# RWKV scan: the transposed operands and the place of a chunk's decay

## The chip, the cores and the metric

The kernel runs on one core of one Trainium2 chip. The metric is the device time of one execution in microseconds; before the change it is 4066.91 us, the median of three runs (4065.96 to 4070.18).

## The reference, cut to what matters

The program is three model blocks one after the other. The change touches one part of the second block, a recurrence of the RWKV-7 kind over 512 tokens, run forward and backward over 16 heads of width 64. With a state S per head, a decay w, a key k, a "removal" key kk and gains b, what is computed per token is

```
S_t = diag(w_t) S_{t-1} - (S-side term built from kk_t and b_t) + k_t v_t^T
y_t = S_t^T r_t          (forward and backward results are added)
```

The kernel does this by chunks of 64 tokens. Inside a chunk everything becomes products of matrices. From chunk to chunk the state moves by one affine step, S' = phi S + psi. With D the product of the decays of a whole chunk, one value per row of the state, both forms below give the same step:

```
before:  phi = diag(D) + (tail operands)^T (...)      psi = (tail operands)^T (...)
after:   S' = D * ( (eye + (side operands)^T (...)) S )  +  D * ( (side operands)^T (...) )
```

A tail operand is k or b times the decay from its token to the end of the chunk; a side operand is k or b divided by the decay up to its token. The first is D times the second.

## The kernel before

`rwkv_projection` makes the operands; at its end it also prepares the first half of the scan (`first_half`), beside its matmuls. `rwkv_scan` then runs 16 halves: u = 0 to 15, tile u // 2 of 128 channels (two heads), forward where u is even and backward where it is odd. Each engine (PE, DVE, ACT) has its program as a loop over u, with the order of the steps written out by hand: the early work of half u is woven between the late work of half u - 1 (its state steps and outputs). I call one pass of that loop a turn and number it by u, so a forward turn has u even. An engine never goes past an instruction that waits, so the written order is also the order of time. `need(u, name, n)` waits for the n-th event of that name of half u.

What the change and the prediction touch, by lines:

- DVE `summed` L3264 (running sum of log decays), `exponents` L3273 (total minus running sum), `keys` L3282, `sides` L3288 and L3289 (`scan_KB`, the side operands), `rows_read` L3297, `past` L3432, `tails` L3304 and L3305 (`scan_hat`, the tail operands).
- DVE `masked` L3313: copies the Gram matrices out of PSUM, `scan_MH` for the first set (w = 0) and `scan_NG` for the second (w = 1). PE `grams` L2933 makes them.
- DVE `crossed` L3369 (`scan_Z`) and `carried` L3380 (`scan_X`), PE `crossed` L2972, `carried` L2984 and `turned` L2947: the doubling levels 3, 4 and 5 of the block inverse; ACT `turned` L3189 (`scan_Y`).
- DVE `substituted` L3350 and L3353, and `blocks_placed` L3362, which starts the doubling of half u.
- PE `tail_rows` L2915: transposes of `scan_hat`, which ACT copies to `scan_tok`; PE `values` L3086.
- PE `transitions` L3021 to L3027, DVE `transitions` L3389 (phi), ACT `decay_diagonals` L3172 (`scan_diag`), ACT `offsets` L3181 (psi).
- PE `state_step` L3062 and DVE `state_step` L3421, six times per half; PE `within` L3040 to L3046 lies between the first and the second of them, and PE `turned(u, 2)` L2947 behind the second.

The order on PE from the Gram matrices to the start of the doubling is: `grams(u, 0)`, `carried(u-1, 5)`, `tail_rows(u)`, `values(u)` (forward only), `turned(u-1, 5)`, `solved(u-1)`, `grams(u, 1)`, `spread_blocks(u)`, `transitions(u-1)`, `values_carried(u)`, `bonus_sums(u)` (forward only), `state_step(u-1, 1)`, `within(u-1)`, `state_step(u-1, 2)`, `turned(u, 2)`. The end of a turn on DVE is `keys`, `crossed(u, 4)`, `sides`, `carried(u, 4)`, `rows_read`, `past`, `tails`, `crossed(u, 5)`, and the next turn opens with `masked(u+1, 0)`, then `carried(u, 5)`.

Of the kernel before, what the change touches and what calls it, by code (L numbers as in the profile page):

```python
# [14 lines left out]
P = 128  # L15
SEQ = 512
# [2370 lines left out]
def rwkv_projection(G, T):  # L2387
# [17 lines left out]
    with ExitStack() as ctx:  # L2405
# [4 lines left out]
                  "scanned", "opened", "exponents", "inverse_exp", "exps", "prepared", *(f"staged_out_{m}" for m in range(KT)))  # L2410
# [153 lines left out]
        def _(act):  # L2564
# [62 lines left out]
            for s in range(KT + 1, STEPS):  # L2627
# [14 lines left out]
                if s == 2 * KT + 3:  # L2642
                    act.wait_ge(S["exponents"], 1)
                    act.activation(T.pe_end[:, FWD, :], F[:, RW_CHUNK - 1::RW_CHUNK], ACT.Exp, scale=DECAY_SCALE)
                    act.activation(inv, F, ACT.Exp, scale=-DECAY_SCALE).then_inc(S["inverse_exp"], 1)
                if s == 2 * KT + 4:
                    act.activation(upto(grown), by_chunk(F), ACT.Exp, scale=DECAY_SCALE)
                    act.activation(upto(left), upto(left), ACT.Exp, scale=DECAY_SCALE).then_inc(S["exps"], 1)
# [5 lines left out]
        def _(dve):  # L2654
# [36 lines left out]
            def first_half(m):  # L2691
# [5 lines left out]
                if m == 2:  # L2697
                    total = F[:, RW_CHUNK - 1::RW_CHUNK]
                    total = bass.AP(tensor=total.tensor, offset=total.offset, ap=[total.ap[0], total.ap[1], [0, RW_CHUNK]])
                    dve.wait_ge(S["scanned"], 1)  # L2700
                    dve.tensor_tensor(upto(left), total, by_chunk(F), ALU.subtract).then_inc(S["exponents"], 1)
# [6 lines left out]
                if m == 6:  # L2708
# [4 lines left out]
                    dve.tensor_tensor(by_chunk(T.hat[:, 0, :]), by_chunk(ld[:, 1, :]), upto(left), ALU.mult)  # L2713
                if m == 7:
                    dve.tensor_tensor(by_chunk(T.hat[:, 1, :]), by_chunk(ld[:, 3, :]), upto(left), ALU.mult)
# [75 lines left out]
def rwkv_scan(G, T):  # L2791
# [11 lines left out]
    PER = dict(scanned=1, exponents=1, edge=1, sums_read=2, exps=1, keys_ready=1, rows_ready=1, sides_ready=1, tails_ready=1, token_sum=3, token_done=3, gram_sum=4, gram_done=4,  # L2803
               z_sum=3, z_done=3, x_sum=3, x_done=4, y_sum=4, y_done=4,
               block_masked=3, compacted=1, unit=1, spread_sum=1, spread_done=1, product=SUB - 1, small=SUB - 1, nv_sum=1, nv_done=1,
               ua_sum=2, ua_done=2, diag_done=1, phi_sum=2, phi_done=2, psi_done=2, own_sum=1, own_done=1, read_done=1,
               state_sum=6, state_done=6, past_sum=1, past_done=1)
    PER_TURN = dict(decays_loaded=16, loaded=16, bonus_in=1, bonus_sum=1, bonus_done=1, bonus_stored=16, v_sum=1, v_done=1)
    with ExitStack() as ctx:
# [4 lines left out]
        AR, KB, hat, masks, bonus, pe_end = T.AR, T.KB, T.hat, T.masks, T.bonus, T.pe_end  # L2814
        diag = G.sb("scan_diag", [P, 2, N_CHUNKS, RW_N], ctx=ctx)
# [46 lines left out]
        def _(sp):  # L2862
# [5 lines left out]
            for i in range(KT):  # L2868
                if i == 1:
                    sp.wait_ge(S["v_spilled"], 16 * 2)  # L2870
                if i:
# [6 lines left out]
                    need(2 * i - 1, "tails_ready", 1)  # L2878
# [8 lines left out]
        def _(pe):  # L2887
# [17 lines left out]
            def tail_rows(u):  # L2905
# [144 lines left out]
            def state_step(u, n):  # L3050
# [76 lines left out]
        def _(act):  # L3127
            need = needer(act)

            def decays(u):  # L3130
# [3 lines left out]
                need(u, "exponents", 1)  # L3134
                ends = F[:, RW_CHUNK - 1::RW_CHUNK]
                if d == FWD:
                    act.sem_inc(S["edge"], 1)
                else:
                    act.activation(left[:, :, 0:1], ends.rearrange("p (c t) -> p c t", t=1), ACT.Copy).then_inc(S["edge"], 1)
                act.activation(pe_end[:, d, :], ends, ACT.Exp, scale=DECAY_SCALE).then_inc(S["sums_read"], 1)  # L3140
                act.activation(upto(grown), by_chunk(F), ACT.Exp, scale=DECAY_SCALE)
                need(u, "edge", 1)
                act.activation(by_chunk(inv), by_chunk(F) if d == FWD else ahead(left), ACT.Exp, scale=-DECAY_SCALE).then_inc(S["sums_read"], 1)
                need(u, "sums_read", 2)
                of = upto(left) if d == FWD else left
                act.activation(of, of, ACT.Exp, scale=DECAY_SCALE).then_inc(S["exps"], 1)
# [18 lines left out]
            def decay_diagonals(u):  # L3165

# [8 lines left out]
            def offsets(u):  # L3175
                if not 0 <= u < HALVES:
                    return
                d = u % 2
# [44 lines left out]
            act.sem_inc(S["edge"], 1)  # L3223
            act.sem_inc(S["sums_read"], 2)
            act.sem_inc(S["exps"], 1)
            for u in range(-1, HALVES + 1):
# [11 lines left out]
                decay_diagonals(u)  # L3238
# [4 lines left out]
        def _(dve):  # L3243
# [22 lines left out]
            def exponents(u):  # L3266
                if not 0 <= u < HALVES:
                    return
# [30 lines left out]

            def tails(u):  # L3300
                if not 0 <= u < HALVES:
                    return
# [1360 lines left out]
```

## Time and profile before

| | us |
|---|---|
| median of three runs | 4066.91 |
| the profiled execution | 4058.67 |
| its span | 4057.3 |
| PE busy | 3854.9 (95%) |
| DVE busy | 2282.2 (56%) |
| ACT busy | 1318.3 (32%) |
| the scan, from the first masked Gram matrix to its last output | 1777 to 2170 |

The scan is 393 us of the span, about a tenth. A share of busy time is a mean over stages that are limited by different engines, so what the change is worth can be read only inside these 393 us, and there from what each engine waits for. Of the views used below, the one by stretch gives busy time and granted clock, the one of waits gives who waited for whom, the one of groups gives the mean duration of a kind of instruction, and the instructions in order of time show which wait ends last. An idle time in brackets stands behind the instruction that ended it, with what released it.

### The profile page before, as it was taken

Reading aid. Unit: us, or ns where it says so; the run is one execution under the profiler, and the core shown is the slowest. Engines: PE = TensorE matmul, PEld = TensorE weight load, DVE = VectorE, ACT = ScalarE, POOL = GpSimd, SP = SyncE. Lnnn points to the kernel's source line nnn. Section 1 sums busy time; section 2 is a strip of 40 time slices with the busy share of each in tenths; the row PEclk is TensorE's granted clock in tenths of the full one; section 3 lists DMA queues with packets and bytes.
Section 4 is the critical chain, followed back from the end, with each engine's and each line's share of the span. In section 5 each row is a group of like instructions: output and inputs, shape, how many; then the busy total and the mean of one; then the engine's idle time right before and its main releaser. Section 6 shows DMA issues by size and latency. Waiting matters only on the chain. (4 is left out here: it accounts for less than half of the span.)

```text
span 4057.3 us, 63395 instructions
## 1 busy us (share of the span) xinstructions
PE 3854.9 (95%) x26412; PEld 3044.2 (75%) x26412; DVE 2282.2 (56%) x3290; ACT 1318.3 (32%) x2121; POOL 1348.0 (33%) x550
## 2 busy tenths in 40 slices
PE   8999999999999999988888999999999999999998
PEld 6856788876778887577775788777777787877886
DVE  5746477567677665568884776465550626251033
ACT  3246233343223332444443433322222112103222
POOL 1001444443234441000001444355554343654442
PEclk9999999999999999999998999999999999999998
DMA  5310222232112223441112222222122112222221
GB/s 176 125 50 35 93 94 99 88 132 104 62 63 104 103 83 111 160 151 45 49 45 87 83 89 98 90 83 83 67 79 75 66 63 90 88 104 83 101 86 62
DMA packets 43375, 359.85 MB, mean 89 GB/s; under 512 B 4307, under 2 KB 4691, under 8 KB 23804
## 3 DMA queue, kind: packets, MB, share of 16 engines
q1 hardware_dynamic: 43132, 356.35, 24.3%
q8 instruction: 184, 3.01, 0.3%
q14 instruction: 59, 0.48, 0.0%
HBM read 333.79 MB, written 22.28 MB: 88 GB/s over the span
## 5 line engine op out<-in xcount | busy, mean ns | idle before, releaser
L352 POOL TENSOR_TENSOR ffn_weights_low<-weight_ring,ffn_weights_high 128x2048 fp32r<-128x2048 f32 x128 | 591.8, 4624 | 787.3 <-ACT ffn_weights_high L451 786.6
L202 PE MATMUL banks<-ffn_in_high,ffn_weights_low 128*128 128x512 f32 x2048 | 800.8, 391 | 12.8 <-POOL ffn_weights_low L352 8.8
L203 PE MATMUL banks<-ffn_in_low,ffn_weights_high 128*128 128x512 f32 x2048 | 798.2, 390 | 0.0
L204 PE MATMUL banks<-ffn_in_high,ffn_weights_high 128*128 128x512 f32 x2048 | 798.2, 390 | 0.0
L202 PEld LDWEIGHTS banks<-ffn_in_high,ffn_weights_low 128*128 128x128 f32 x2048 | 385.4, 188 | 98.9 <-POOL ffn_weights_low L352 11.3
L204 PEld LDWEIGHTS banks<-ffn_in_high,ffn_weights_high 128*128 128x128 f32 x2048 | 385.3, 188 | 80.6
L203 PEld LDWEIGHTS banks<-ffn_in_low,ffn_weights_high 128*128 128x128 f32 x2048 | 385.3, 188 | 80.0 <-issue 0.7
L451 ACT ACTIVATE ffn_weights_high<-weight_ring 128x2048 fp32r<-128x2048 f32 x128 | 245.2, 1915 | 560.0 <-PE banks L204 560.0
L605 DVE SCALAR_TENSOR_TENSOR ffn_gate<-ffn_up,columns_sb,ffn_gate 128x511 f32<-128x511 f32 (+1 forms) x132 | 273.6, 2072 | 160.8 <-ACT ffn_value L495 160.8
L3764 POOL TENSOR_TENSOR third_weights_low<-weight_ring,third_weights_high 128x1024 fp32r<-128x1024 f32 x144 | 359.8, 2498 | 11.5
L3762 POOL CAST third_weights_high<-weight_ring 128x1024 fp32r<-128x1024 f32 x144 | 159.4, 1107 | 512.4 <-PE banks L204 483.4
L202 PE MATMUL banks<-third_x_high,third_weights_low 128*128 128x512 f32 x768 | 311.5, 406 | 2.0 <-DVE merge_gate L4582 0.9
L204 PE MATMUL banks<-third_x_high,third_weights_high 128*128 128x512 f32 x768 | 300.6, 391 | 0.0
L203 PE MATMUL banks<-third_x_low,third_weights_high 128*128 128x512 f32 x768 | 300.1, 391 | 0.0
L626 DVE TENSOR_TENSOR ffn_in_low<-ffn_hidden,ffn_in_high 128x512 fp32r<-128x512 f32 x80 | 165.9, 2121 | 138.4 <-ACT ffn_in_high L509 138.4
L3528 POOL TENSOR_TENSOR rwout_weights_low<-weight_ring,rwout_weights_high 128x1024 fp32r<-128x1024 f32 x8 | 18.6, 2361 | 615.6 <-ACT rwout_weights_high L3579 615.6
L202 PEld LDWEIGHTS banks<-third_x_high,third_weights_low 128*128 128x128 f32 x768 | 145.1, 189 | 32.5 <-issue 3.1
L204 PEld LDWEIGHTS banks<-third_x_high,third_weights_high 128*128 128x128 f32 x768 | 144.7, 188 | 31.1
L203 PEld LDWEIGHTS banks<-third_x_low,third_weights_high 128*128 128x128 f32 x768 | 145.2, 189 | 27.8 <-issue 1.0
L202 PE MATMUL banks<-first_in_high,first_weights_low 128*128 128x512 f32 x336 | 139.5, 415 | 15.7 <-DVE first_in_low L1105 12.5
L498 ACT ACTIVATE ffn_gate<-ffn_gate 128x512 f32<-128x512 f32 x66 | 41.8, 634 | 320.3 <-DVE ffn_gate L605 320.3
L618 DVE TENSOR_TENSOR ffn_hidden<-ffn_gate,banks 128x512 f32 (+1 forms) x22 | 15.2, 689 | 215.7 <-ACT ffn_gate L500 215.7
(646 smaller groups left out, 7474.4 us busy)
## 6 DMA issues: line engine op xcount, KB each, us to landing
weight_ring<-weights SPq DMA_DIRECT2D x144, 2048.0 KB, 7.7
scan_in<-rwkv_operands SPq DMA_DIRECT2D x7, 1280.0 KB, 5.8
rwkv_operands<-rwin_staged SPq DMA_DIRECT2D x23, 256.0 KB, 3.3
scan_in<-rwkv_operands SPq DMA_DIRECT2D x8, 512.0 KB, 3.9
bias_tiles<-bias_rows SPq DMA_DIRECT2D x8, 448.0 KB, 8.9
residual<-x SPq DMA_DIRECT2D x4, 512.0 KB, 7.1
hyena_u_x_T<-decay SPq DMA_DIRECT2D x2, 1024.0 KB, 8.0
rwkv_residual<-residual SPq DMA_DIRECT2D x1, 2048.0 KB, 7.2
```

The costliest lines, as they stand in the source:

```text
L202: pe.matmul(out, w[1], x[0], start=start, stop=False, skip_group_check=True)
L203: pe.matmul(out, w[0], x[1], start=False, stop=False, skip_group_check=True)
L204: return pe.matmul(out, w[0], x[0], start=False, stop=stop, skip_group_check=True)
L352: pool.tensor_tensor(parts[1], landed, parts[0].bitcast(F32), ALU.subtract).then_inc(S["split"], 1)
L451: act.activation(parts[0], landed, ACT.Copy).then_inc(S["rounded"], 1)
L498: act.activation(gc[:, h, :], gc[:, h, :], act_func).then_inc(S["activated"], 1)
L605: ins = dve.scalar_tensor_tensor(out=buf[:, h, to], in0=up_scaled[:, h, q, of], scalar=G.col(taps, 8 * t + 4 * q + tap), in1=buf[:, h, to] ...
L618: dve.tensor_tensor(gT[:, t, :], gc[:, h, :], G.banks[:, b + 1, :], ALU.mult).then_inc(S["hidden"], 1)
L626: dve.tensor_tensor(parts[1], gT[:, t, :], parts[0].bitcast(F32), ALU.subtract).then_inc(S["tile_split"], 1)
L3528: pool.tensor_tensor(w_parts[1][:, k, :], landed(k), w_parts[0][:, k, :].bitcast(F32), ALU.subtract).then_inc(S["split"], 1)
L3762: pool.tensor_copy(parts[0], landed).then_inc(S["rounded"], 1)
L3764: pool.tensor_tensor(parts[1], landed, parts[0].bitcast(F32), ALU.subtract).then_inc(S["split"], 1)
```

## The change

The side operands are transposed in place of the tail operands, so `tails` and the tile `scan_hat` go, as do the forward half's `exponents` and the exponential that fed it. `scan_diag` and the eight ACT instructions that fill it go; phi is now formed by adding the plain identity. The chunk's decay D (`pe_end`) enters at two places: ACT copies psi in eight pieces of 64 columns, each scaled by its chunk's D, where it copied two pieces of 256; and each DVE state step becomes (product times D) plus psi, a three-operand instruction. PE's first state step now waits for five pieces of psi. In `rwkv_projection` the same tail work of the first half goes.

```diff
-                need(u, "tails_ready", 1)
+                need(u, "sides_ready", 1)
                 if u > 1:
-                    need(u - 2, "psi_done", 2)
+                    need(u - 2, "psi_done", N_CHUNKS)
...
-                        mm = pe.transpose(B(d, 2 + n)[:, j * P:(j + 1) * P], hat[:, n, j * P:(j + 1) * P], G.con("ident"))
+                        mm = pe.transpose(B(d, 2 + n)[:, j * P:(j + 1) * P], KB[:, n, j * P:(j + 1) * P], G.con("ident"))
...
                 if n == 1:
                     need(u, "phi_done", 2)
-                    need(u, "psi_done", 2)
+                    need(u, "psi_done", N_CHUNKS // 2 + 1)
...
-                for c in range(N_CHUNKS):
-                    ins = act.activation(diag[:, d, c, :], eye, ACT.Copy, scale=pe_end[:, d, c:c + 1])
-                ins.then_inc(S["diag_done"], 1)
...
-                for p in range(2):
-                    need(u, "phi_done", p + 1)
-                    act.activation(psi[:, p::2, :], B(d, 2 + p)[:, 256:512].rearrange("p (j k) -> p j k", j=JT), ACT.Copy)\
+                for c in (*order[d][1 - d::2], *order[d][d::2]):
+                    need(u, "phi_done", 2 - c % 2)
+                    at = 256 + c // 2 * RW_N
+                    act.activation(psi[:, c, :], B(d, 2 + c % 2)[:, at:at + RW_N], ACT.Copy, scale=pe_end[:, u % 4, c:c + 1])\
                        .then_inc(S["psi_done"], 1)
...
             def exponents(u):
-                if not 0 <= u < HALVES:
+                if not 0 <= u < HALVES or u % 2 == FWD:
...
-            def tails(u):
-                if not 0 <= u < HALVES:
-                    return
-                behind = upto(left) if u % 2 == FWD else ahead(grown)
-                dve.tensor_tensor(by_chunk(hat[:, 0, :]), by_chunk(k), behind, ALU.mult)
-                dve.tensor_tensor(by_chunk(hat[:, 1, :]), by_chunk(b), behind, ALU.mult).then_inc(S["tails_ready"], 1)
...
-                need(u, "diag_done", 1)
-                for p in range(2):
+                for p in (1, 0):
                     need(u, "phi_sum", p + 1)
-                    dve.tensor_tensor(phi[:, p::2, :], B(d, 2 + p)[:, 0:256].rearrange("p (j k) -> p j k", j=JT), diag[:, d, p::2, :], ALU.add)\
+                    dve.tensor_tensor(phi[:, p::2, :], B(d, 2 + p)[:, 0:256].rearrange("p (j k) -> p j k", j=JT), spread(eye, JT), ALU.add)\
...
-                if n == 1:
-                    need(u, "psi_done", 2)
-                dve.tensor_tensor(state[:, d, n + 1, :], B(d, 3)[:, n * RW_N:(n + 1) * RW_N], psi[:, order[d][n], :], ALU.add)\
-                   .then_inc(S["state_done"], 1)
+                need(u, "psi_done", N_CHUNKS // 2 + 1 + n // 2)
+                c = order[d][n]
+                dve.scalar_tensor_tensor(out=state[:, d, n + 1, :], in0=B(d, 3)[:, n * RW_N:(n + 1) * RW_N], scalar=pe_end[:, u % 4, c:c + 1],
+                                         in1=psi[:, c, :], op0=ALU.mult, op1=ALU.add).then_inc(S["state_done"], 1)
```

ACT's `decays` for a forward half loses the last of its exponentials; `pe_end` gets four slots in place of two; an unused tile of the size of `scan_hat` keeps the addresses of what follows. The loads of the next tile's operands (SP) no longer wait for the tail operands.

## Rows read from the trace of the kernel before

**Rows 1.** Busy time by stretch, whole scan: PE, PEld, DVE, ACT, POOL, clock, DMA share, GB/s.

```profile
1777.00:2170.00 393.00, 322.75 (x10427) 277.69 (x10420) 304.40 (x792) 173.44 (x430) 1.36 (x1) 0.93 0.15 52
```

**Rows 2.** Waits, 1800 to 2150: us in total, times, longest us.

```profile
DVE scan_state L3421 <- PE banks L3062: 26.6, 34, 2.0
...
PE banks L3062 <- ACT scan_psi L3181: 8.5, 7, 1.4
...
PE banks L3062 <- issue: 4.5, 8, 1.3
```

**Rows 3.** In order of time, into backward turn 7: start us, us, engine, line.

```profile
1941.87 1.08 PE L2933 MATMUL banks<-scan_AR,scan_KB 64*64 64x128 f32 x32
...
1942.06 0.68 DVE L3305 TENSOR_TENSOR scan_hat<-scan_in,residual 128x512 f32<-128x512 f32 x1
1942.67 0.42 DVE L3369 TENSOR_TENSOR scan_Z<-banks,scan_masks_sb 128x256 f32<-128x256 f32 x1
...
1943.01 1.29 DVE L3313 TENSOR_TENSOR scan_MH<-banks,scan_masks_sb 128x512 f32<-128x512 f32 x2
...
1944.21 0.41 DVE L3380 TENSOR_TENSOR scan_X<-scan_X,banks 128x256 f32<-128x256 f32 x1
```

**Rows 4.** In order of time, the same place in forward turn 8.

```profile
1963.04 1.10 PE L2933 MATMUL banks<-scan_AR,scan_KB 64*64 64x128 f32 x32
...
1964.49 0.67 PE L2984 MATMUL banks<-scan_Z,scan_Y 64*64 64x32 f32 x32 [0.34 <-DVE scan_Z L3369]
...
1965.54 0.41 DVE L3380 TENSOR_TENSOR scan_X<-scan_X,banks 128x256 f32<-128x256 f32 x1
...
1966.45 0.60 PE L2947 MATMUL banks<-constants_sb,scan_X 128*128 128x128 f32 x4
```

**Rows 5.** In order of time, turn 7, the second set of Gram matrices.

```profile
1947.01 1.09 PE L2933 MATMUL banks<-scan_AR,scan_KB 64*64 64x128 f32 x32
...
1947.54 0.69 DVE L3273 TENSOR_TENSOR residual<-residual 128x512 f32<-128x512 f32 x1
...
1948.15 1.29 DVE L3313 TENSOR_TENSOR scan_NG<-banks,scan_masks_sb 128x512 f32<-128x512 f32 x2
```

**Rows 6.** In order of time, DVE: the first masked Gram matrix of the scan.

```profile
1777.39 1.29 DVE L3313 TENSOR_TENSOR scan_MH<-banks,scan_masks_sb 128x512 f32<-128x512 f32 x2 [9.89 <-PE banks L2933]
```

**Rows 7.** Groups on ACT by shape, the scan: count, busy us, mean ns.

```profile
L3189 ACT ACTIVATE scan_Y<-banks 128x512 f32<-128x512 f32 x64 | 38.2, 597 | 106.8 <-PE banks L2947 106.8
L3172 ACT ACTIVATE scan_diag<-scan_masks_sb,scan_decay 128x64 f32<-128x64 f32 x128 | 32.1, 336 | 0.0
...
L3181 ACT ACTIVATE scan_psi<-banks 128x256 f32<-128x256 f32 x32 | 10.7, 396 | 3.4 <-DVE scan_phi L3389 3.4
```

**Rows 8.** In order of time, ACT: psi of one half, the diagonals of another.

```profile
1951.61 0.67 ACT L3181 ACTIVATE scan_psi<-banks 128x256 f32<-128x256 f32 x2
...
1959.29 2.00 ACT L3172 ACTIVATE scan_diag<-scan_masks_sb,scan_decay 128x64 f32<-128x64 f32 x8
```

**Rows 9.** In order of time, turn 7: first state step to the start of the doubling.

```profile
1952.38 0.33 PE L3062 MATMUL banks<-scan_psi,scan_phi 64*64 64x64 f32 x4 [1.36 <-ACT scan_psi L3181]
...
1953.69 0.68 DVE L3362 TENSOR_TENSOR scan_X<-scan_small,scan_masks_sb 128x512 f32<-128x512 f32 x1
...
1954.43 0.66 PE L2947 MATMUL banks<-constants_sb,scan_X 128*128 128x128 f32 x4 [0.15 <-DVE scan_X L3362]
```

**Rows 10.** In order of time, PE: the same place in turns 1 and 15.

```profile
1812.08 0.22 PE L3062 MATMUL banks<-scan_state,scan_phi 64*64 64x64 f32 x1
...
1812.39 0.66 PE L2947 MATMUL banks<-constants_sb,scan_X 128*128 128x128 f32 x4
...
2140.27 0.33 PE L3062 MATMUL banks<-scan_state,scan_phi 64*64 64x64 f32 x4
2140.53 0.66 PE L2947 MATMUL banks<-constants_sb,scan_X 128*128 128x128 f32 x4
```

**Rows 11.** In order of time, DVE: a three-operand instruction with a scalar per partition.

```profile
1954.45 0.74 DVE L3254 SCALAR_TENSOR_TENSOR scan_bonus<-scan_in,columns_sb 128x512 f32<-128x512 f32 x1
```

More of the change, by code:

```diff
@@ L2409, in rwkv_projection @@
                   "mixed_out", "gained_out", "key_in", "decays_in", "reset_in", "masks_in", "first_share", "first_key", "first_gain", "first_read",
-                  "scanned", "opened", "exponents", "inverse_exp", "exps", "prepared", *(f"staged_out_{m}" for m in range(KT)))
+                  "scanned", "opened", "inverse_exp", "exps", "prepared", *(f"staged_out_{m}" for m in range(KT)))
         sb = lambda name, shape, dt=F32: G.sb("rwin_" + name, shape, dt, ctx=ctx)
@@ L2642, in _ @@
                 if s == 2 * KT + 3:
-                    act.wait_ge(S["exponents"], 1)
-                    act.activation(T.pe_end[:, FWD, :], F[:, RW_CHUNK - 1::RW_CHUNK], ACT.Exp, scale=DECAY_SCALE)
+                    act.wait_ge(S["scanned"], 1)
+                    act.activation(T.pe_end[:, 0, :], F[:, RW_CHUNK - 1::RW_CHUNK], ACT.Exp, scale=DECAY_SCALE)
                     act.activation(inv, F, ACT.Exp, scale=-DECAY_SCALE).then_inc(S["inverse_exp"], 1)
                 if s == 2 * KT + 4:
-                    act.activation(upto(grown), by_chunk(F), ACT.Exp, scale=DECAY_SCALE)
-                    act.activation(upto(left), upto(left), ACT.Exp, scale=DECAY_SCALE).then_inc(S["exps"], 1)
+                    act.activation(upto(grown), by_chunk(F), ACT.Exp, scale=DECAY_SCALE).then_inc(S["exps"], 1)
             for m in range(KT):
@@ L2696, in first_half @@
                     dve.tensor_tensor_scan(F, G.x[:, RESET_TILE, :], ld[:, 5, :], 0.0, ALU.mult, ALU.add).then_inc(S["scanned"], 1)
[L2697 to L2701, printed above, removed]
                 if m == 5:
@@ L2813, in rwkv_scan @@
         NG = G.sb("scan_NG", [P, 2, 2, JT, 2, RW_CHUNK], ctx=ctx)
-        AR, KB, hat, masks, bonus, pe_end = T.AR, T.KB, T.hat, T.masks, T.bonus, T.pe_end
-        diag = G.sb("scan_diag", [P, 2, N_CHUNKS, RW_N], ctx=ctx)
+        AR, KB, masks, bonus, pe_end = T.AR, T.KB, T.masks, T.bonus, T.pe_end
         phi = G.sb("scan_phi", [P, N_CHUNKS, RW_N], ctx=ctx)
@@ L3133, in decays @@
                 d = u % 2
-                need(u, "exponents", 1)
                 ends = F[:, RW_CHUNK - 1::RW_CHUNK]
                 if d == FWD:
-                    act.sem_inc(S["edge"], 1)
+                    need(u, "scanned", 1)
+                    act.activation(pe_end[:, u % 4, :], ends, ACT.Exp, scale=DECAY_SCALE).then_inc(S["sums_read"], 1)
+                    act.activation(inv, F, ACT.Exp, scale=-DECAY_SCALE).then_inc(S["sums_read"], 1)
+                    act.activation(upto(grown), by_chunk(F), ACT.Exp, scale=DECAY_SCALE).then_inc(S["exps"], 1)
                 else:
+                    act.wait_ge(S["exponents"], u // 2 + 1)
                     act.activation(left[:, :, 0:1], ends.rearrange("p (c t) -> p c t", t=1), ACT.Copy).then_inc(S["edge"], 1)
[L3140 to L3146, printed above, removed]
+                    act.activation(pe_end[:, u % 4, :], ends, ACT.Exp, scale=DECAY_SCALE).then_inc(S["sums_read"], 1)
+                    act.wait_ge(S["edge"], u // 2 + 1)
+                    act.activation(by_chunk(inv), ahead(left), ACT.Exp, scale=-DECAY_SCALE).then_inc(S["sums_read"], 1)
+                    need(u, "sums_read", 2)
+                    act.activation(left, left, ACT.Exp, scale=DECAY_SCALE).then_inc(S["exps"], 1)
             def key_rows(u):
@@ L3237, in _ @@
                 turned(u, 3)
-                decay_diagonals(u)
                 key_rows(u + 1)
@@ L3440, in bonus_times_value @@
                    .then_inc(S["bonus_done"], 1)
-            for sem in ("keys_ready", "rows_ready", "sides_ready", "tails_ready", "bonus_in", "scanned", "exponents"):
+            for sem in ("keys_ready", "rows_ready", "sides_ready", "bonus_in", "scanned"):
                 dve.sem_inc(S[sem], 1)
@@ L3472, in _ @@
                 past(u - 1)
-                tails(u + 1)
                 crossed(u, 5)
```

21 lines of the change are left out of this document (6 added, 15 removed).

## The prediction

> **What bounds the kernel now.** I read the stretches first, to find the scan and its clock: in 393 us PE is busy for 323 and DVE for 304 [rows 1], so both are near full and neither share says which one a turn waits for. The reader is to see that "DVE at 77%" does not yet make DVE work worth removing. Then the waits: inside the scan DVE stands 26.6 us in 34 waits for the product of a state step, and PE waits for psi before its first state step in 7 turns, with 8 more where the profile names no releaser [rows 2]; in those 8 too PE's step starts 0.1 us after ACT's second psi copy ends, so all 15 full turns wait for psi there. Last, the instructions in order of time, at the three places that the change touches.
>
> The first place is the end of a turn. DVE finishes the tail operands, masks scan_Z and starts scan_MH at 1943.01, and PE's Gram matrices end at 1941.87 + 1.08 = 1942.95 [rows 3]. scan_MH starts 0.06 us behind the Gram matrices, which is what a release takes. So although DVE works without a gap, it is PE that lets it go on. I read the same pair at all turns: the distance is 0.01 to 0.11 in thirteen of the fifteen turns from 1 on, and 0.21 in turns 8 and 10. The second place is the second set of Gram matrices: PE ends them at 1948.10, scan_NG starts at 1948.15 [rows 5], and this distance is 0.02 to 0.08 in all sixteen. The third is the way from psi to the doubling: PE's step at 1952.38, then `within`, the second step, and the transposes that start the doubling [rows 9]. The loop that sets the time thus runs through PE and ACT, and through DVE in the substitution, the state steps and from the sixth step to the fourth-level scan_X.
>
> **The tail operands (L3304, L3305) go.** Two instructions of 0.68 that follow one another at 0.60 [rows 3]: 1.2 us of DVE in each turn. What they hold back is scan_Z of level 5 and what follows it. In a backward turn scan_MH can't start sooner than the Gram matrices end, and scan_X stands behind it on DVE (1944.21), so PE's transposes of scan_X, and all behind them, come no sooner: worth 0. In a forward turn PE has work of its own between (`tail_rows`, `values`): scan_X ends at 1965.95, but the transposes start at 1966.45 [rows 4], so here PE's queue counts, and it starts with `carried` at 1964.49, 0.34 us idle behind scan_Z. With scan_Z early it starts at about 1964.05, where the Gram matrices let it go: 0.45 gained. That is the most of the seven forward turns; in the least it is 0, since `carried` already follows the Gram matrices. I take half: 7 x 0.23 = 1.6 us gained; the bounds are 0 and 3.2.
>
> **The forward exponents (L3273) go**, 0.69 on DVE once in two turns, and stand ahead of scan_NG. scan_NG is released by PE [rows 5]: worth 0. The exponential that ACT loses there only makes ACT idle sooner. The transposes wait for the side operands in place of the tail operands; both are ready before PE gets there, and SP's load of the next tile is issued sooner, with nobody waiting for it.
>
> **In the projection** the same work goes. DVE then stands idle for 9.89 us until the first Gram matrices are there [rows 6]: worth 0.
>
> **The diagonals (L3172) go**, eight of 0.336 us, 2.0 together [rows 8], between two ACT copies with idle time before the next: worth 0. The identity in their place has the same shape on DVE: 0, and I see no reason for either sign.
>
> **Psi in eight pieces.** This is the part that lies on the path. Two copies take 0.67 from the start of the first to the end of the second [rows 8]. Now PE waits for five pieces. A piece has the shape and the scalar operand of a diagonal, 0.336 each, eight in 2.00, so one follows the other at (2.00 - 0.336) / 7 = 0.238, and the fifth ends after 4 x 0.238 + 0.336 = 1.29: 0.62 later than now. The other bound leaves the scalar operand out: from 597 at 512 elements and 396 at 256 [rows 7] a copy costs 0.785 ns per element, 0.245 at 64, following one another at about 0.13, so 0.77 in all: 0.10 later. I take 0.62, since the diagonal is the nearer row: same size, same scale operand, same engine, only its input is in SBUF.
>
> The Trainium skill (VectorE: DVE Perf Modes, the section on the TRN2 errata) speaks against this part: it says that the fixed cost is paid by every instruction, and that many small tiles pay it each time. The rows agree, since a quarter of the elements takes 336 against 396. The same section puts the fixed part lower when the input is in PSUM, and with its figures, plus what ScalarE: Activation LUTs (the section on what ACT_TABLE_LOAD costs) gives for a scalar operand per partition, I would estimate the fifth piece 0.4 later in place of 0.62, and the sum below 3 us lower.
>
> How much of it reaches the doubling? In turn 7 scan_X is placed at 1953.69 + 0.68 = 1954.37 and the transposes wait for it [rows 9]; PE had been ready 0.27 earlier, so 0.62 - 0.27 = 0.35 is left. Turns 2 and 11 look alike. In the other twelve PE is the late one: its transposes follow the second state step by 0.31 in turn 1 and 0.26 in turn 15, the first and the last of them [rows 10], and the whole 0.62 passes. Sum: 12 x 0.62 + 3 x 0.35 = 8.5; with the lower bound 12 x 0.10 = 1.2. What is late next is DVE's second step, its bonus and own output behind it, and then scan_Z of level 3: the same delay by another way, so none of it is given back. ACT itself is held 1.3 us longer by eight pieces; its next copy, scan_Y, stands idle for 106.8 us in 64 copies [rows 7], 1.7 each, and moves by 0.6 itself: I hold it covered, closely in the forward turns.
>
> **State steps with three operands.** Of this kind a 512-element instruction takes 0.74 [rows 11] against 0.68 without the scalar [rows 3]: 0.06 more each. A third of the steps make DVE wait for PE [rows 2] and others lie in DVE's full stretches; I take three of six on the path: 15 x 3 x 0.06 = 2.7; the bounds are 0 and 5.4. Nothing here excludes that the small size hides it.
>
> **The last pass**, half 15 alone, has nothing beside it: 0.62 + 6 x 0.06 = 1.0.
>
> **The sum**: - 1.6 + 8.5 + 2.7 + 1.0 = +10.6 us. The profiled execution took 4058.67 and would take 4069.3. It is 8.2 below the median of the runs, so I add the sum to the median: 4077.5. Some of PE's stalls without a releaser come from the supply of its instructions, I believe, and a longer wait just ahead of one may swallow part of it; I round down to 4077. The low bounds of the terms give -3.2 + 1.2 + 0.1 = -2, the high ones 8.5 + 5.4 + 1.0 = +15, that is 4065 to 4082.
>
> **The rivals.**
>
> A. DVE's relief counts after all (faster). If DVE and not PE were last at the end of a turn, each turn would win the 1.2 us of the tails and each second one 0.6 of the exponents: 15 x 1.2 + 7 x 0.6 = 22, less the 12 that the rest costs: -10, 4057. For it speaks that DVE shows no idle time through most turn ends; against it the distances of 0.06 and 0.05 [rows 3, 5]. It decides from the point where DVE ends its work there after PE in most turns, which it now does clearly in two.
>
> B. The psi pieces are cheap (same). If a piece costs what the lower bound says, and the state steps nothing more: 1.2 + 0.1 - 1.6 = -0.3, or +3 if the state steps do cost their 2.7 and 0.4: 4067 to 4070. For it: input in PSUM. Against it: the diagonals.
>
> C. PE's clock (slower by more). The granted clock is 0.93 in the scan [rows 1], which is 0.07 x 2 x 393 = 55 us at 1.2 GHz in place of 2.4. PE's wait before the first step, 1.36 in turn 7 [rows 9], grows by 0.6. If the time at 1.2 GHz grows by a quarter with it, 14 us at half the rate cost at most 7 more: 4084. It can also fall the other way.
>
> **How the numbers follow.** The forecast has 0.50, A 0.10, B 0.25, C 0.15. Range: the forecast's own 4065 to 4081, opened towards C above and halfway to A below: 4062 to 4087. A measurement can tell about 0.2%, 8.1 us, from no change, so "same" is 4058.8 to 4075.0. B lies in it whole, and of the forecast a quarter: 0.25 + 0.12 = 0.37; faster is A, 0.10; slower is the rest, 0.53.
>
> **What would show each step.** In the changed trace: scan_MH and scan_NG still start 0.05 behind the Gram matrices while DVE shows about 1 us of new idle time before them (if they start earlier than PE's end allows now, A). ACT's L3181 line has 128 instructions of 64 columns; their mean and the time from the first to the end of the fifth settle 0.10 against 0.62. PE's L3062 starts 0.1 behind the fifth piece, and its wait is some 0.6 longer. The state step's mean on DVE goes from 0.222 to about 0.28. The clock of 1777 to 2170 tells of C. I am wrong if the scan's 393 us [rows 1] fall, or if the time that moves lies outside them.

## The result, and the profile after

| | before | after |
|---|---|---|
| median of 17 runs each, us | 4066.84 | 4074.53 |
| the profiled execution's span | 4057.3 | 4066.4 |
| the scan, first scan_MH to the end of its last output | 389.8 | 397.4 |

The ratio is 1.0020, with a 95% interval of 1.0013 to 1.0027: 5 to 11 us slower, 7.7 between the medians. On another chip the same pair gave 1.0008 (0.9999 to 1.0018), 3.3 us between the medians. Within the profiled executions the scan takes 7.5 us longer. So DVE's and ACT's work went down and the time went up, by 0.1 to 0.3%. The forecast was +10.6, 4077.

The page of the changed kernel, busy time by engine:

```profile
PE 3857.2 (95%) x26412; PEld 3043.6 (75%) x26412; DVE 2265.5 (56%) x3250; ACT 1295.6 (32%) x2073; POOL 1347.2 (33%) x550
```

DVE works 16.7 us less, ACT 22.7 us less, PE 2.3 us more. The scan alone, by stretch, with the same columns as [rows 1]:

```profile
1775.52:2172.88 397.36, 320.68 (x10416) 279.70 (x10416) 289.15 (x754) 149.65 (x380) 0.00 (x0) 0.92 0.15 51
```

Waits between 1800 and 2160 (us in total, times, longest), the answer to [rows 2]:

```profile
DVE scan_state L3393 <- PE banks L3051: 28.7, 39, 1.8
...
PE banks L3051 <- ACT scan_psi L3163: 11.8, 7, 1.8
PE banks L3051 <- issue: 9.5, 9, 1.8
...
DVE scan_MH L3286 <- PE banks L2922: 7.0, 14, 0.6
```

PE now waits up to 1.8 us ahead of a first state step (before: 1.4). And DVE, relieved of the tails and the forward exponents, stands idle in 14 turns for the Gram matrices, most of which it used to reach just in time. The end of a turn shows it, in order of time on DVE, against [rows 3]:

```profile
1939.24 0.42 DVE L3342 TENSOR_TENSOR scan_Z<-banks,scan_masks_sb 128x256 f32<-128x256 f32 x1 [0.62 <-PE banks L2961]
1940.12 1.29 DVE L3286 TENSOR_TENSOR scan_MH<-banks,scan_masks_sb 128x512 f32<-128x512 f32 x2 [0.46 <-PE banks L2922]
```

Where the tail operands stood there are 0.62 + 0.46 = 1.1 us of idle time, and the 1.2 us taken away have bought nothing in this turn. From a forward turn (10), PE in order of time, against [rows 4]:

```profile
2011.40 1.10 PE L2922 MATMUL banks<-scan_AR,scan_KB 64*64 64x128 f32 x32
2012.30 0.65 PE L2973 MATMUL banks<-scan_Z,scan_Y 64*64 64x32 f32 x32
```

Here `carried` follows the Gram matrices without a gap. Before, 0.34 us lay between in turns 8 and 10, but 0.14 or less in the other five forward turns, 1.0 us in all seven; now it is 0.16 in turn 8 and nothing in the others. I found no other place where the relief reaches PE.

Psi and the first state step, by shape and in order of time, against [rows 7] to [rows 9]:

```profile
L3163 ACT ACTIVATE scan_psi<-banks,scan_decay 128x64 f32<-128x64 f32 x128 | 28.0, 346 | 3.6 <-DVE scan_phi L3361 3.6
```
```profile
1949.24 1.75 ACT L3163 ACTIVATE scan_psi<-banks,scan_decay 128x64 f32<-128x64 f32 x8
```
```profile
1950.48 0.33 PE L3051 MATMUL banks<-scan_psi,scan_phi 64*64 64x64 f32 x4 [1.85 <-ACT scan_psi L3163]
```

PE's step starts 1950.48 - 1949.24 = 1.24 us behind the start of the first piece; it was 0.77 in turn 7 before (1952.38 - 1951.61). So 0.47 us are added, and the wait of 1.36 has become 1.85. Summed over the 16 first state steps, in the group of PE by line (idle time before it, and its releasers), first before and then after:

```profile
L3062 PE MATMUL banks<-scan_psi,scan_phi 64*64 64x64 f32 x64 | 5.9, 254 | 14.3 <-ACT scan_psi L3181 9.8 <-issue 4.5
```
```profile
L3051 PE MATMUL banks<-scan_psi,scan_phi 64*64 64x64 f32 x64 | 5.6, 242 | 21.9 <-ACT scan_psi L3163 13.6 <-issue 8.3
```

14.3 has become 21.9: 7.5 us more, before rounding. I call this sum the first-step wait. PE's step starts 0.10 us behind the end of the piece that it needs in all 16 halves of both traces, also where the profile names no releaser. The state step on DVE, by shape:

```profile
L3393 DVE SCALAR_TENSOR_TENSOR scan_state<-banks,scan_decay,scan_psi 128x64 f32<-128x64 f32 x96 | 27.0, 281 | 33.2 <-PE banks L3051 32.4
```

0.281 where two operands took 0.222.

### The profile page after: what moved, and what is told of

The parts are those of the page before. It is cut to its first block and busy times, and to the rows that moved or that the text cites. A ratio compares the mean times of both kernels' runs of the same rounds, so it can differ in the third digit from the quotient of the medians.

```text
span 4066.4 us, 63367 instructions
## 1 busy us (share of the span) xinstructions
PE 3857.2 (95%) x26412; PEld 3043.6 (75%) x26412; DVE 2265.5 (56%) x3250; ACT 1295.6 (32%) x2073; POOL 1347.2 (33%) x550
## 5 line engine op out<-in xcount | busy, mean ns | idle before, releaser
L202 PEld LDWEIGHTS banks<-ffn_in_high,ffn_weights_low 128*128 128x128 f32 x2048 | 384.9, 188 | 98.6 <-POOL ffn_weights_low L352 11.3
```

Source lines behind the costliest of these rows:

```text
L202: pe.matmul(out, w[1], x[0], start=start, stop=False, skip_group_check=True)
```

## The experiments

The theory was that the eight pieces are what costs, and that the DVE relief is hidden. The rivals were that PE's clock, or the supply of PE's own instructions, makes the difference. The ratios below are to the kernel before on the same chip. The runs were made on three chips, so two kernels are compared directly only where the text says that they shared one. I call the last three versions v1, v2 and v3.

**One part alone: the pieces**, on the kernel before.

```diff
-                    need(u, "psi_done", 2)
+                    need(u, "psi_done", N_CHUNKS // 2 + 1)
...
+                for c in (*order[d][1 - d::2], *order[d][d::2]):
+                    need(u, "phi_done", 2 - c % 2)
+                    at = 256 + c // 2 * RW_N
+                    act.activation(psi[:, c, :], B(d, 2 + c % 2)[:, at:at + RW_N], ACT.Copy, scale=reset[:, 1:2])\
+                       .then_inc(S["psi_done"], 1)
```

> The kernel before with one part alone of the change: psi is copied in eight pieces of 64 columns, each with a scale operand per partition (a one), in the order of the change, and PE's first state step waits for five of them. Theory (the pieces are what lengthens the turn): PE's wait before its first state step grows from 1.36 to 1.83 us in backward turns and from 0.3 to 0.77 in forward ones, as in the changed kernel, and of these 16 x 0.47 = 7.5 us between 4 and 7 reach the end: 4071 to 4074. Rival (PE's clock or the supply of its instructions makes the difference, not the pieces): the waits grow, but the time stays within 2 us of 4067.

Measured: 1.0009 (1.0000 to 1.0017), that is 0 to 7 us, middle 3.7. The first-step wait is 21.8 us, as with the change. The middle lies just under the 4 to 7 us that the theory expected, and the interval doesn't exclude the rival's 2 us. Alone it settles only that the waits are the change's waits.

**The other part alone: three operands**, on the kernel before.

```diff
-                dve.tensor_tensor(state[:, d, n + 1, :], B(d, 3)[:, n * RW_N:(n + 1) * RW_N], psi[:, order[d][n], :], ALU.add)\
-                   .then_inc(S["state_done"], 1)
+                dve.scalar_tensor_tensor(out=state[:, d, n + 1, :], in0=B(d, 3)[:, n * RW_N:(n + 1) * RW_N], scalar=reset[:, 1:2],
+                                         in1=psi[:, order[d][n], :], op0=ALU.mult, op1=ALU.add).then_inc(S["state_done"], 1)
```

> The kernel before with the other part alone: each DVE state step is a three-operand instruction (product times a one, plus psi). Theory: a step takes 0.284 in place of 0.224 us; with three of six on the path the time grows by 2.7, to 4069.5, with 0 to 5.4 as bounds. Rival (all six count, since a third of the steps make DVE wait and the others lie where DVE has no gap): +5.5, 4072.5.

Measured: 1.0004 (0.9994 to 1.0013), -2 to +5 us; a step takes 0.282. And the reverse, on the changed kernel, with an addition in place of the three operands (the chunk's decay is left out of the state step):

> The changed kernel with the state step on DVE a two-operand addition (the chunk's decay is left out of the state step; psi keeps it). A step takes 0.224 in place of 0.284 us, 5.8 us of DVE time in all. Theory (three of six steps on the path): 2.7 us under the changed kernel, which is at 1.0015 of the kernel before on average so far: 1.0008. Rival 1 (all on the path): 5.4 under it, 1.000. Rival 2 (PE's queue covers them): no difference, 1.0015.

Measured: 1.0011 (1.0001 to 1.0021), where the changed kernel was at 1.0008 on one chip and 1.0020 on another. Neither tells 2.7 from 0. That all six steps lie on the path, 5.4 us, is just outside the interval of the first, and the second can't exclude it, since its chip had no run of the changed kernel.

**The DVE work put back** into the changed kernel: both multiplications at the place of the tail operands, and the forward exponents, read by nobody. (The loads of the next tile wait for them again, as before the change.)

```diff
-                if not 0 <= u < HALVES or u % 2 == FWD:
+                if not 0 <= u < HALVES or u < 0:
...
+                dve.tensor_tensor(by_chunk(T.hat[:, 0, :]), by_chunk(k), by_chunk(inv), ALU.mult)
+                dve.tensor_tensor(by_chunk(T.hat[:, 1, :]), by_chunk(b), by_chunk(inv), ALU.mult).then_inc(S["tails_ready"], 1)
```

> The changed kernel with the DVE work of before put back: two multiplications of 512 columns a turn at the place of the tail operands and the forward halves' exponents (nobody reads either). 15 x 1.2 + 7 x 0.6 = 22 us of DVE work. Theory (it was hidden behind PE): only the forward turns lose their gain, +1.6 to +2 over the changed kernel, 4076 to 4077. Rival (DVE's relief counted and paid for a part of the pieces): +10 or more, 4085.

Measured: 1.0011 (1.0003 to 1.0020). The changed kernel without this work:

> The changed kernel itself, beside the others on this chip. Both theories: 1.001 to 1.003 of the kernel before.

1.0008 (0.9999 to 1.0018), just under what was expected. The two ran on different chips, each beside the kernel before; the difference of the ratios says that 22 us of DVE work cost 1 us, give or take 5. Against the 1.0020 of the first pair it is -4, give or take 5. Neither leaves room for the rival's 10 or more: the relief was hidden. In its trace the idle time before scan_MH shrinks again (1777 to 2165; the first turn's is not in it):

```profile
L3295 DVE TENSOR_TENSOR scan_MH<-banks,scan_masks_sb 128x512 f32<-128x512 f32 x30 | 19.3, 686 | 4.4 <-PE banks L2923 4.1
```

The same group of the changed kernel has 8.1 us.

**A much longer wait**, on the kernel before: the pieces halved to 32 columns, and all sixteen waited for.

```diff
-                    need(u, "psi_done", 2)
+                    need(u, "psi_done", 2 * N_CHUNKS)
...
+                    for k in range(2):
+                        at = 256 + c // 2 * RW_N + k * 32
+                        act.activation(psi[:, c, k * 32:(k + 1) * 32], B(d, 2 + c % 2)[:, at:at + 32], ACT.Copy, scale=reset[:, 1:2])
```

> The kernel before with psi in sixteen pieces of 32 columns (scale operand a one), and PE waits for all sixteen: 15 x 0.17 + 0.3 = 2.9 us in place of 0.67, so 2.2 us more in each of the 16 passes, 36 us in all. Theory 1 (the wait is on the path and passes through, less 0.27 in three turns): +34 to +36, 4097 to 4100 where the kernel before is 4063.6. Theory 2 (a wait gives PE's instruction supply time to catch up, so part of it is paid back in fewer stalls): +22 to +30, with the stalls without a releaser outside the first state step clearly under their 17 us.

Measured: 4108.25 us, 1.0107 (1.0090 to 1.0123): 37 to 50 us more. The group of PE's first state steps:

```profile
L3062 PE MATMUL banks<-scan_psi,scan_phi 64*64 64x64 f32 x64 | 6.5, 281 | 51.0 <-ACT scan_psi L3183 33.4 <-issue 17.6
```

The first-step wait grew by 51.0 - 14.3 = 36.7 us, and the scan of the profiled execution by 426.7 - 389.8 = 36.9. The time measured, 37 to 50 us more over six runs, lies above both theories. Theory 2's +22 to +30 is excluded as a total, but its sign came true, as the stalls outside the first state steps fell from 17.3 to 11.6. What made up for them is the clock. In turn 2, the stretch from the first state step to the start of the doubling, by stretch:

```profile
1839.41:1842.67 3.26, 3.26 (x104) 3.14 (x104) 0.82 (x2) 1.78 (x5) 0.00 (x0) 0.51 0.02 5
```

The granted clock there is 0.51, so nearly all of it ran at 1.2 GHz, behind a wait of 2.60 us; in the kernel before the same stretch took 2.29 us at 1.00. Over turns 1 to 15 these stretches lasted 40.9 us, 31.6 of them at 1.2 GHz; in the kernel before it was 34.5, with 6.4. That the total equals the wait is the sum of two opposite effects, not a wait that passes untouched.

**The wait shortened again**, on the changed kernel: two copies of 256 columns, without the decay (the factor D on psi is left out of the computation).

```diff
-                for c in (*order[d][1 - d::2], *order[d][d::2]):
...
+                for p in (1, 0):
+                    need(u, "phi_done", 2 - p)
+                    act.activation(psi[:, p::2, :], B(d, 2 + p)[:, 256:512].rearrange("p (j k) -> p j k", j=JT), ACT.Copy)\
+                       .then_inc(S["psi_done"], 1)
```

> The changed kernel with psi copied by two instructions of 256 columns again and without its decay (the factor D on psi is left out of the computation; everything else is as in the changed kernel). PE's wait before its first state step goes back by 0.47 us a turn, 7.5 us in all. Theory 1 (the wait is on the path and passes through): 5 to 7 us under the changed kernel, at or below the kernel before. Theory 2 (PE's own supply of instructions sets much of the time there, so a shorter wait ahead comes back as stalls without a releaser behind it): 1 to 4 us under the changed kernel, and the stalls without a releaser outside the first state step grow from 16 to 18 us or more.

Measured: 0.9998 (0.9989 to 1.0007), that is 4 us under the changed kernel on the same chip, at theory 2's upper end and a little under theory 1's 5 to 7. The first-step wait is 14.3 again, as before the change, but the stalls for which the profile names no releaser ("issue"), outside the first state steps, are 25.0 us in place of 17.5. The 4 us are uncertain by about 5, so the time alone doesn't separate the theories. With two copies the changed kernel is back at the time of the kernel before, within 0.1%; together with the sixteen pieces this is the best evidence that the pieces are what costs. The stalls, however, don't follow from the wait alone: the kernel before has the same 14.3 us of wait, and only 17.3 and 19.5 us of them in its two traces.

**A version with no psi but the first**, on the changed kernel. The product of a state step is added in PSUM to the raw offset, and DVE multiplies by D on the way out.

```diff
+                    mm = pe.matmul(B(d, 2 + c % 2)[rows[h], at:at + RW_N], phi[rows[h], c, :], of, start=False, stop=True, skip_group_check=True)
...
+                dve.tensor_scalar(state[:, d, n + 1, :], B(d, 2 + c % 2)[:, at:at + RW_N], pe_end[:, u % 4, c:c + 1], None, ALU.mult)
```

> The changed kernel, where the product of a state step is added in PSUM onto the raw offset of its chunk, and DVE multiplies the sum by the chunk's decay on the way out (one two-operand instruction with a scale). So only the first chunk's psi is copied by ACT, and PE's first state step waits for one piece in place of five. The same function is computed. Theory (the wait for psi is on the path): PE's wait is 0.8 us shorter than in the changed kernel, 0.33 shorter than before; the start of the doubling is then held by DVE's substitution in most turns, so 0.3 to 0.6 a turn is gained against the changed kernel: 4065 to 4070, with DVE's step also back to some 0.23 us. Rival (clock and supply of instructions rule): 4072 to 4076 as with the change.

Measured: 1.0001 (0.9992 to 1.0011). It does not compute the same function after all: each offset in `transitions` begins with a start flag of its own, and by the next version's result the last such flag in a bank leaves the earlier columns marked for overwriting. So most state steps (by the order of the products, five of six) replace the offset that they should add to. The next version gives the flag to the first product of each bank and row group alone:

```diff
-                                  tok[rows[p], d, 1, j, rows[h]], start=True, stop=True)
+                                  tok[rows[p], d, 1, j, rows[h]], start=(j == 0), stop=True, skip_group_check=True)
...
-                                  vt[rows[p], u // 2 % 2, j, rows[h]], start=True, stop=False, skip_group_check=True)
+                                  vt[rows[p], u // 2 % 2, j, rows[h]], start=False, stop=False, skip_group_check=True)
```

> As v1_psum_accumulation, with the start flag only on the first product of each PSUM bank and row group, so that a later flag doesn't make the state steps overwrite the offsets they are to be added to. The order and number of instructions are those of v1. Theory 1 (what PE waits for psi passes through): 0.8 us less wait a turn than with the change gives 4 to 8 us under the changed kernel, so below the kernel before by 0 to 3. Theory 2 (supply of instructions): as v1, at the kernel before, +-2, with 25 us or more of stalls without a releaser outside the first state step.

Measured: 4064.18, 0.9995 (0.9986 to 1.0003): 5 us under the changed kernel on its chip by the ratios, for 12.4 us less wait. The other stalls are 25.3. Both theories' numbers touch it.

Last, the one psi copy stands ahead of the copy of the carried values, and phi's additions begin with the bank of the first chunk.

```diff
-                for p in (1, 0):
+                for p in (d, 1 - d):
...
+                offsets(u - 1)
                 values_carried(u)
-                offsets(u - 1)
```

> v2_psum_accumulation with ACT's one psi copy ahead of its copy of the carried values, released by the first of the two phi additions, which now starts with the bank that holds the first chunk. PE's wait ahead of the first state step should go from 1.0 to about 0.6 us in backward turns and from 0.45 to near 0 in forward ones, some 5 to 7 us in all against v2. Theory 1 (waits pass through): 3 to 6 us under v2_psum_accumulation, 4058 to 4062 where the kernel before is at 4066. Theory 2 (PE's supply of instructions and DVE's substitution take over, since the doubling can't start before DVE has placed its blocks): within 2 us of v2, the other stalls without a releaser over 28 us.

Measured: 4061.64, 0.9994 (0.9985 to 1.0003): 2.7 us under the kernel before, though the interval holds no change too. Beside the kernels before on their chips v3 is where v2 was (0.9995), though it waits 5.4 us less: theory 1's 3 to 6 us under v2 did not come, but intervals of this width can't exclude them. Its first-step wait is 4.0 us, 10 less than before the change. Where did these 10 go? The two groups of PE, the first state steps and `within` directly behind them:

```profile
L3029 PE MATMUL banks<-scan_NG,scan_v 64*64 64x64 f32 x512 | 27.2, 228 | 6.7 <-issue 6.7
...
L3053 PE MATMUL banks<-scan_psi,scan_phi 64*64 64x64 f32 x64 | 5.8, 243 | 4.0 <-ACT scan_psi L3165 3.8 <-issue 0.3
```

`within` of the changed kernel, whose first-step wait is 21.9:

```profile
L3029 PE MATMUL banks<-scan_NG,scan_v 64*64 64x64 f32 x512 | 25.6, 233 | 0.0
```

and of the kernel before, 14.3:

```profile
L3040 PE MATMUL banks<-scan_NG,scan_v 64*64 64x64 f32 x512 | 28.2, 240 | 1.8 <-issue 1.6
```

With 51.0 us of wait the stall ahead of this group is 0.0, with 21.9 it is 0.0, with 14.3 it is 1.8, with 4.0 it is 6.7. One turn of v3, in order of time, has such a stall in the middle of `within`, among products whose operands had long been there:

```profile
1950.05 0.33 PE L3053 MATMUL banks<-scan_psi,scan_phi 64*64 64x64 f32 x4 [0.50 <-ACT scan_psi L3165]
1950.18 0.28 PE L3029 MATMUL banks<-scan_NG,scan_v 64*64 64x64 f32 x2
1951.40 0.28 PE L3029 MATMUL banks<-scan_NG,scan_v 64*64 64x64 f32 x3 [0.94 <-issue]
```

**From the first state step to the doubling.** How much of a wait arrives is seen at the next point that others wait for, PE's transposes at the start of the doubling. Turn 1 before, whose doubling starts at 1812.39 [rows 10], and its two ends after, PE in order of time:

```profile
1810.20 0.27 PE L3062 MATMUL banks<-scan_psi,scan_phi 64*64 64x64 f32 x2 [1.37 <-ACT scan_psi L3181]
```
```profile
1808.72 0.27 PE L3051 MATMUL banks<-scan_psi,scan_phi 64*64 64x64 f32 x2 [1.83 <-ACT scan_psi L3163]
...
1810.50 0.66 PE L2936 MATMUL banks<-constants_sb,scan_X 128*128 128x128 f32 x4
```

The wait is 0.46 longer, and the way behind it is 1.78 in place of 2.19, 0.41 shorter, with the same products following one another more closely. Most turns look like this. In others the doubling was held by DVE before: scan_X ends 0.06 ahead of it in 3 of 15 turns in one trace of the kernel before and in 7 in the other, with eight pieces in none. The mean of this distance, over those of turns 1 to 15 that lie wholly at 2.4 GHz, by the number of psi copies waited for:

| psi | traces | first step to doubling, us |
|---|---|---|
| one copy | v1, v2, v3 | 2.39, 2.42, 2.54 |
| two copies | before, again, three operands, after with two copies | 2.16, 2.09, 2.10, 2.16 |
| five of eight pieces | before with pieces, after, again, DVE work back, two operands | 1.84, 1.81, 1.85, 1.81, 1.81 |
| sixteen pieces | before with sixteen pieces (3 turns only) | 1.78 |

With eight pieces PE waits 0.47 longer and then reaches the doubling 0.3 sooner, so some 0.2 a turn is left at its start, about 3 us in all. That agrees with the 3.7 us of the pieces alone and the 4 us of the return to two copies. In no trace is the distance under 1.78, so a wait that grows further has nothing left to be set against.

**All traces together.** For each I summed, from the first scan_MH to the end of the scan's last output, the first-step wait, PE's other idle time ascribed to "issue", and the time that the trace's record of the granted clock gives at 1.2 GHz:

| kernel | scan | first-step wait | other "issue" | at 1.2 GHz |
|---|---|---|---|---|
| before | 389.8 | 14.3 | 17.3 | 51.9 |
| before, again | 385.8 | 14.6 | 19.5 | 32.2 |
| before, three operands | 392.6 | 14.4 | 19.5 | 54.7 |
| before, pieces | 393.5 | 21.8 | 17.6 | 43.4 |
| before, sixteen pieces | 426.7 | 51.0 | 11.6 | 76.9 |
| after | 397.4 | 21.9 | 17.5 | 60.9 |
| after, again | 403.6 | 21.9 | 18.7 | 70.7 |
| after, DVE work back | 400.1 | 21.8 | 22.2 | 49.9 |
| after, two operands | 397.2 | 21.8 | 20.0 | 54.1 |
| after, two copies | 393.3 | 14.3 | 25.0 | 36.3 |
| v1 | 395.4 | 9.1 | 27.0 | 54.1 |
| v2 | 389.2 | 9.5 | 25.3 | 39.1 |
| v3 | 387.6 | 4.0 | 27.6 | 46.0 |

A fit of the ten traces that I had by then gave: scan = 340 + 1.0 x wait + 1.1 x other stalls + 0.3 x time at 1.2 GHz. The last three of the runs were held against it:

> The kernel before itself, for a second trace of it. Both theories: 1.000 of itself within 0.001. From the traces so far the scan's length is 340 us plus PE's wait ahead of the first state steps, plus 1.1 of its other stalls without a releaser, plus 0.3 of its time at 1.2 GHz: this trace should obey that within 2 us, with 14.3 us of wait ahead of the first state steps.

Measured: 0.9997 (0.9988 to 1.0006), with a wait of 14.6. Its scan should be 340 + 14.6 + 1.1 x 19.5 + 0.3 x 32.2 = 385.7, and is 385.8. v3 comes out 0.6 shorter than the rule says, the two-operand kernel 2.8 shorter, more than the 2 us that I had allowed. The rule is bookkeeping in large part: the scan is PE's busy plus PE's idle time, wait and stalls are two parts of the idle time, and the rest of it is 26.7 to 28.6 us in all traces. Coefficients near one follow from that alone and don't show that a wait costs its whole length. What the rule tells beyond this is the last term, since PE's busy time alone goes by 316 + 0.25 x the time at 1.2 GHz, within 3 us. The clock differs between traces of one and the same kernel by 20 us (51.9 and 32.2). It stands in [rows 1] as 0.93, and in the row of "before, again" as 0.96:

```profile
1778.11:2163.88 385.77, 313.62 (x10416) 270.31 (x10416) 304.11 (x791) 171.00 (x427) 0.00 (x0) 0.96 0.16 53
```

## Why the prediction was right, point by point

The sign, the range and what costs were right: +10.6 forecast, +7.7 measured, 4074.5 in 4062 to 4087. The size is in part luck. The second chip gave +3.3, and the largest term was too high twice over, in the length of the wait and in how much of it arrives, while other parts, of which more time at 1.2 GHz may be one, came on top. By "over 0.2%" (4075.0) the result lies just inside "same", which had 0.37 against 0.53 for slower. (The working gives 4082 as the upper bound of the sum and 4081 where it sets the range; nothing hangs on it.)

- **What bounds a turn.** Right. scan_MH still starts 0.03 to 0.06 behind the Gram matrices in all turns but one, where the records overlap, and DVE shows the idle time that was forecast. The distance between a start and its release in the kernel before told it, while DVE showed no gap there.
- **The tail operands, worth 1.6.** Consistent. From the start of scan_MH to the first substitution, turns 1 to 14 sum to 98.6 us before and 96.8 after; over all traces the kernels with this DVE work average 98.6 and the four of the change's form without it 97.7 (v1, v2 and v3: 97.9, 99.3, 97.6). So about 1, which is no more than traces of one form differ by. Rival A (22 us of relief, -10 in all) is out, by the kernel with the work put back.
- **The projection, the diagonals, the forward exponents, all 0.** Nothing speaks against it. In the scan the rule above serves kernels with and without them within 3 us. The projection lies ahead of the scan: that starts at 1775.6 to 1779.7 in the five traces with its tail work and at 1772.9 to 1779.3 in the eight without. Only the forward exponents were tested by a run, together with the tails.
- **Psi in pieces, 0.62 a turn.** Too high by a quarter; the mis-sized term is the distance between two pieces. A piece lasts 0.346, as the diagonal's 0.336, but eight take 1.75, so (1.75 - 0.346) / 7 = 0.20 and not 0.238 from one to the next; the fifth ends 0.47 later than before. The row behind it was of copies that read SBUF, these read PSUM. The estimate from the figures of the Trainium skill (VectorE: DVE Perf Modes, the section on the TRN2 errata, with ScalarE: Activation LUTs, the section on what ACT_TABLE_LOAD costs) was 0.4, nearer to the measured 0.47 than my row. The Trainium skill says there of inputs in SBUF that many small tiles pay the fixed cost each time, and its table has a fixed part for PSUM inputs too. The trace agrees: out of PSUM, a quarter of the elements takes 346 ns (with the scale operand) against 396 (without). The 336 of the prediction was of an SBUF input, so its pair didn't show this.
- **How much of it passes.** Wrong in size. I let 0.27 be absorbed in three turns and the whole pass in twelve, "none of it given back". The wait did grow in all 16 halves, by 7.5 us in place of 9.9 (16 x 0.62). But in the turns at full clock 0.3 of each 0.47 was given back before the doubling, in part where DVE had been late, as I had said but in more turns, and in part because PE's products follow one another more closely behind a longer wait, which I had not looked for. About 3 us are left in place of 8.5 + 0.6. I had this possibility in the sum, as a rounding of half a microsecond.
- **State steps, 2.7.** The price of one is right (0.06). That three of six lie on the path isn't shown by either experiment; anything from 0 to about 5 fits them.
- **ACT covered.** Its eight pieces delay the next copies, but the first scan_Y behind them still has 0.51 us or more of idle before it in all 15 turns of both traces of the changed kernel (0.93 or more before). Closely in the forward turns too, and covered.
- **Rival B** (pieces nearly free) falls with the 0.47. **Rival C** (the clock): the time at 1.2 GHz is 52, 32, 55 and 36 us in the traces with 14.3 to 14.6 us of wait, 43 to 71 in those with 21.8, and 77 with 51.0. It tends to grow with the wait, and in the sixteen-piece kernel it stands right behind it, so part of C may be in the result: the 9 us more of the traced pair cost 2 to 3 by the rule. But two traces of one kernel differ by 20, so for eight pieces this is not shown.

The account is then about 3 (what is left of the wait) + 2 to 3 (clock, if it is one) + 0 to 5 (state steps) - 1 (relief), so 4 to 10 against a measured 5 to 11, and 3.3 on the second chip. That the traced pair's scan grew by 7.5, just as its wait did, is then a coincidence of parts.

What stays open: what holds PE back where the profile says "issue". That it is the supply of PE's instructions fits what is seen (it strikes amid products that wait for nothing, and within `within` it is less behind a long wait), but I found no run that would show it. Open too is why the kernels of the changed form with little wait have 25 us or more of such stalls, 5 or more above the kernel before; in the one with two copies most of the difference lies outside `within` and the state steps.

## What to carry to other kernels

Before taking work off an engine, look at the distance between the end of what releases its next step and that step's start: DVE showed hardly a gap at the end of a turn, and still it was PE that released it in thirteen of fifteen turns. Splitting one copy into many is paid where someone waits for the first few, here 0.47 us of wait a turn, and was not repaid by 39 us less work on DVE and ACT. And a wait is not worth its length. Follow the queue on to the next point that others wait for: here 0.3 of the 0.47 was made up for before that point, and of 10 us less wait in v3 nearly all reappeared as stalls in the same queue. A much longer wait had nothing left to be set against, and the clock behind it was lower.

## What the runs showed of the hardware that I had not expected

A wait ahead of PE's first state steps changes what lies behind it. At 2.4 GHz the way from there to the doubling takes 2.4 to 2.5 us behind the shortest waits, 2.1 to 2.2 behind those of the kernel before, and 1.8 behind those that are 0.47 longer. Behind waits of 2.6 to 3.7 us, in the sixteen-piece kernel, PE was granted 1.2 GHz for 31.6 of 40.9 us of that way; behind those of 0.3 to 1.4 us in the kernel before, for 6.4 of 34.5.

On ACT, a copy of 64 columns out of PSUM with a scale per partition follows its predecessor by 0.20 us, one out of SBUF by 0.238, at nearly the same duration (0.346 and 0.336). On DVE, instructions of 64 columns out of PSUM take 0.281 us with a scale per partition, whether it is the product with the scale alone (v2) or product and sum, and the plain sum without one takes 0.222. And a matmul's start flag reaches beyond the columns that it writes: with a flag on every offset of `transitions` (v1) later additions to earlier columns of the bank overwrote them, with one flag for each bank and row group (v2) they added.
